# Two-layer trunk of delta rule, attention and convolution: convolution in pieces, a second home for the masked coupling, memory values with tokens stationary

## The reference, cut to what matters

```python
h = rms_norm(x, norm_pre[layer])
qkv_a, z_a, b_a, g_a, q_b, k_b, v_b, z_b = split_sizes(h @ w_in, AB_SIZES)
qkv_a = silu(causal_depthwise_conv(qkv_a, conv_w))          # 4 taps
# delta rule, chunks of 64 tokens:
n_mat = where(strict, (k_beta @ k.T) * gamma, 0)             # the coupling within a chunk
sol = triangular_solve(eye + n_mat, rhs)                     # u and w
# over the 8 chunks, one after the other:
v_new = u_i - w_i @ state
o = qd_i @ state + qk_i @ v_new
state = state * cd_i + kd_i.T @ v_new
# memory: m = rms_norm(mem, mem_norm[layer]); k, v = split(m @ w_kv, 2)
```

## Time and profile before

| what | value |
|---|---|
| median of 3 runs | 2610.19 us |
| lowest and highest run | 2605.46 and 2610.9 us |
| the profiled execution | 2604.95 us |
| its span, first to last instruction | 2603.2 us |
| mean granted TensorE clock | 0.984 |
| busy share of PE, DVE, ACT, POOL | 95%, 51%, 31%, 12% |

### The profile page before, as it was taken

The page is one execution under the profiler, slowest core; times in us unless marked ns, Lnnn a source line. Parts: engine busy times, 40 slices in busy tenths (PEclk is TensorE's granted clock), DMA queues, the critical chain, the costliest instruction groups (busy, mean ns, idle before and its releaser), DMA issues.

```text
span 2603.2 us, 30751 instructions
## 1 busy us (share of the span) xinstructions
PE 2475.8 (95%) x12244; PEld 2055.0 (79%) x12244; DVE 1315.7 (51%) x1689; ACT 808.6 (31%) x1348; POOL 299.5 (12%) x198
## 2 busy tenths in 40 slices
PE   7999998999999999989989989999999999999986
PEld 6788787878887777978877778888888888887765
DVE  5555545554355656763355575333433343433746
ACT  4232322223244345542233441122212222322442
POOL 3010110202011011001121140000000000010304
PEclk9999999999999999999999989999999999999997
DMA  9522322156355332443321222323232322332212
GB/s 173 88 57 49 66 50 68 45 56 65 51 129 90 65 89 65 154 161 130 96 84 63 76 81 92 101 75 116 91 100 78 114 92 92 98 98 96 73 50 80
DMA packets 222976, 227.76 MB, mean 87 GB/s; under 512 B 9360, under 2 KB 216464, under 8 KB 222864
## 3 DMA queue, kind: packets, MB, share of 16 engines
q1 hardware_dynamic: 222720, 225.64, 34.5%
q10 hardware_dynamic: 144, 0.52, 0.1%
HBM read 221.94 MB, written 4.19 MB: 87 GB/s over the span
## 4 chain that ended last, share of the span: by engine, by line
PE 64%; issue 24%; DVE 5%; POOL 3%; ACT 1%; DMA 1%; SPq 1%; POOLq 0%; ACTq 0%; DVEq 0%
PE acc L797 20%; PE acc L799 19%; PE acc L798 19%; POOL work L1782 2%; DVE weights_lo L1145 1%; DMA weights_raw<-in_ab_w_in 1%; DVE work L1548 1%; PE m L941 1%; PE m L1086 1%; PE m L1098 1%; POOL small L1759 0%; ACT work L719 0%; PE m L1021 0%; DVE input_lo L1561 0%; PE m L776 0%
## 5 line engine op out<-in xcount | busy, mean ns | idle before, releaser
L797 PE MATMUL acc<-input_hi,weights_hi 128*128 128x512 f32 (+1 forms) x3168 | 1242.6, 392 | 53.0 <-DVE weights_lo L1145 22.4
L799 PE MATMUL acc<-input_hi,weights_lo 128*128 128x512 f32 (+1 forms) x3168 | 1214.8, 383 | 1.8 <-issue 1.8
L798 PE MATMUL acc<-input_lo,weights_hi 128*128 128x512 f32 (+1 forms) x3168 | 1213.1, 383 | 0.0
L797 PEld LDWEIGHTS acc<-input_hi,weights_hi 128*128 128x128 f32 x3168 | 601.3, 190 | 188.8 <-issue 35.7
L1145 DVE TENSOR_TENSOR weights_lo<-weights_raw,weights_hi 128x1024 fp32r<-128x1024 f32 x400 | 534.8, 1351 | 374.2 <-ACT weights_hi L409 373.0
L799 PEld LDWEIGHTS acc<-input_hi,weights_lo 128*128 128x128 f32 x3168 | 600.4, 190 | 117.2
L798 PEld LDWEIGHTS acc<-input_lo,weights_hi 128*128 128x128 f32 x3168 | 601.9, 190 | 109.5 <-issue 1.9
L409 ACT ACTIVATE weights_hi<-weights_raw 128x1024 fp32r<-128x1024 f32 x400 | 418.5, 1057 | 617.9 <-PE acc L799 576.9
L1821 POOL TENSOR_TENSOR work<-work 128x512 f32<-128x512 f32 x56 | 72.6, 1296 | 429.0 <-ACT work L671 425.0
L1759 POOL TENSOR_TENSOR small<-small 128x4 f32<-128x4 f32 (+1 forms) x20 | 25.5, 1275 | 741.7 <-DVE small L1329 382.8
L1527 DVE COPY work<-acc 128x512 f32<-128x512 f32 x64 | 41.6, 686 | 134.8 <-PE acc L799 121.6
(11 more groups left out here) (240 smaller groups left out, 1864.9 us busy)
## 6 DMA issues: line engine op xcount, KB each, us to landing
weights_raw<-in_ab_w_in SPq DMA_DIRECT2D x128, 512.0 KB, 5.3
weights_raw<-in_c_w_in SPq DMA_DIRECT2D x128, 512.0 KB, 3.7
weights_raw<-in_m_w_kv SPq DMA_DIRECT2D x32, 512.0 KB, 3.4
weights_raw<-in_ab_w_out SPq DMA_DIRECT2D x32, 512.0 KB, 4.5
weights_raw<-in_m_w_q SPq DMA_DIRECT2D x32, 512.0 KB, 3.3
weights_raw<-in_c_w_out SPq DMA_DIRECT2D x32, 512.0 KB, 3.9
residual<-in_x SPq DMA_DIRECT2D x32, 256.0 KB, 5.2
weights_raw<-in_m_w_o SPq DMA_DIRECT2D x16, 512.0 KB, 3.3
```

What stands on the lines that cost most here:

```text
L797: pe.matmul(out, w_hi[:, o:o + P], hi(kt), start=kt == 0, stop=False)
L798: pe.matmul(out, w_hi[:, o:o + P], lo(kt), start=False, stop=False)
L799: last = pe.matmul(out, w_lo[:, o:o + P], hi(kt), start=False, stop=kt == last_kt)
```

## The change: what it does, and the diff

Six edits go together.
- `convolve` takes its k step: scale and first tap behind step 0, one shifted tap behind each of the steps 1, 2 and 3, always after the replies of that step; the gate of the tile before comes behind step 3. ScalarE's tanh moves one chunk later and to step 1.
- The hops of the delta rule are spread over slots 12 to 60 in place of 12 to 63. `tr`, `dk`, `qb` and `p0` keep their slots (12, 16, 21, 23), `p1` and `y1` go from 26 and 27 to 25 and 26, `y4` and `p5` from 36 and 38 to 35 and 36, `r4` and `s4`, which shared 52, to 49 and 50, `s7` from 59 to 56 and `ft` from 63 to 60.
- The masked coupling is written in turn to `c_t` and to `gam`, which is free once `qb`'s reply has used it. Level 1 now waits for that reply (`qk`), level 2 for `y0`, a later level s for the matmuls of `p` two levels back.
- `value_chunk` projects the values with the memory's tokens as the stationary operand and 256 weight columns moving, so that they come out with tokens on partitions; the transposes and both VectorE copies go.
- ScalarE's `take_values` copies the values to `mv`, scaled by each token's factor: 8 activations in all, ahead of the rest of chunks 12, 16 and 28 and after the last one.
- VectorE's `take_keys` keeps the keys' part.

```diff
@@ -124,3 +124,3 @@
 B_REPLY = {"vt": 1.2, "a": 0.8, "a00": 2.0, "a10": 2.0, "b": 1.2, "b03": 1.8, "b13": 1.8, "f": 0.6}
-D_SLOTS, B_SLOTS = weighted(D_HOPS, 12, 63, D_REPLY), weighted(B_HOPS, 18, 63, B_REPLY)
+D_SLOTS, B_SLOTS = weighted(D_HOPS, 12, 60, D_REPLY), weighted(B_HOPS, 18, 63, B_REPLY)
 C_REPLY = {"s": 5.0, "t": 1.8, "o": 1.5}
@@ -264,2 +264,3 @@
         halves = lambda t: t.rearrange("p (t a n) -> p t a n", a=2, n=CH)
+        level = lambda s: (c_t, gam)[s % 2]
         wq_q = wq.rearrange("p (t n) -> p t n", n=4 * CH)[:, :, CH:3 * CH]
@@ -583,3 +584,3 @@
 
-                    if c == 2:
+                    if c == 3:
                         EA.round(it)
@@ -594,8 +595,8 @@
 
-                    if 1 <= like <= 4 and c < 2:
-                        tanh_conv(it - 1, 2, c)
-                    if like < 4 and c in (8, 9):
-                        tanh_conv(it, 0, c - 8)
-                    if like < 4 and c in (12, 13):
-                        tanh_conv(it, 1, c - 12)
+                    if 1 <= like <= 4 and c in (1, 2):
+                        tanh_conv(it - 1, 2, c - 1)
+                    if like < 4 and c in (9, 10):
+                        tanh_conv(it, 0, c - 9)
+                    if like < 4 and c in (13, 14):
+                        tanh_conv(it, 1, c - 13)
 
@@ -620,3 +621,3 @@
                             projected(c)
-                        if k == 3:
+                        if k == 1:
                             convolved(c)
@@ -652,4 +653,17 @@
 
+            def take_values(q):
+
+                l, j, pair = q // 4, q % 4, P_KV + q
+                act.wait_ge(chunk_used, done_at(pair))
+                act.wait_ge(acc_free, 2 * pair)
+                act.wait_ge(*MG("pow"))
+                for m in range(2):
+                    v0 = (l * 2 + m) * MH * HD + 256 * (j - 2)
+                    act.activation(mv[:, v0:v0 + 256], bank(pair, m, 256), ACT.Copy, scale=t2[:, m:m + 1])\
+                        .then_inc(acc_free, 1)
+
             for c in range(32):
                 split(C_KV + c + 1)
+                if c in (12, 16, 28):
+                    take_values(c // 4 - 1)
                 if 1 <= c <= 8:
@@ -662,2 +676,3 @@
                     split_input(0, xt, C_OUT0, c - 24, c - 23)
+            take_values(7)
 
@@ -871,4 +886,5 @@
                     pe.wait_ge(*GV("y" + str(int(name[1]) - 1), i))
+                    c_s = level(int(name[1]))
                     for h, t in ht:
-                        last = pe.matmul(m(m01, h, t), c_t[:, o(h, t)], inv[:, o(h, t)], start=True, stop=True)
+                        last = pe.matmul(m(m01, h, t), c_s[:, o(h, t)], inv[:, o(h, t)], start=True, stop=True)
                 elif name[0] == "y":
@@ -981,8 +997,20 @@
 
-            def value_transposes(l, j, pair):
+            def value_chunk(g, pair, kt0, l, between):
 
-                pe.wait_ge(*MV(f"vf{l}{j}"))
-                for n in range(4):
-                    last = pe.transpose(acc[2 * (pair % 2)][:, n * P:(n + 1) * P], v_feat[:, n * P:(n + 1) * P], ident)
-                last.then_inc(*MM.did(f"v{l}{j}"))
+                s = g % SPLIT_SLOTS
+                pe.wait_ge(lo_ready, g + 1)
+                if kt0 == 0:
+                    pe.wait_ge(acc_free, 2 * (pair - 1))
+                for k in range(4):
+                    kt = kt0 + k
+                    w = slice(s * CW + k * 256, s * CW + (k + 1) * 256)
+                    for m in range(2):
+                        out = bank(pair, m, 256)
+                        tok = slice(m * P, (m + 1) * P)
+                        pe.matmul(out, mem_h(H_hi, l, kt)[:, tok], w_hi[:, w], start=kt == 0, stop=False)
+                        pe.matmul(out, mem_h(H_hi, l, kt)[:, tok], w_lo[:, w], start=False, stop=False)
+                        last = pe.matmul(out, mem_h(H_lo, l, kt)[:, tok], w_hi[:, w], start=False, stop=kt == KT - 1)
+                    if k == 3:
+                        last.then_inc(chunk_used, 1)
+                    between(k)
 
@@ -1003,3 +1031,3 @@
             for c in range(32):
-                l, q = c // 16, c // 4 - 1
+                l = c // 16
 
@@ -1009,5 +1037,6 @@
                             attn(name, 3)
-                if q >= 0 and c % 4 == 1 and q % 4 >= 2:
-                    value_transposes(q // 4, q % 4, P_KV + q)
                 mem_rms(c)
+                if c % 16 >= 8:
+                    value_chunk(C_KV + c, P_KV + c // 4, 4 * (c % 4), l, between)
+                    continue
                 chunk(C_KV + c, P_KV + c // 4, 4 * (c % 4), KT - 1, width=MEM, between=between,
@@ -1015,3 +1044,2 @@
                       hi=lambda k: mem_h(H_hi, l, k), lo=lambda k: mem_h(H_lo, l, k))
-            value_transposes(1, 3, P_KV + 7)
 
@@ -1337,3 +1365,3 @@
 
-            def convolve(it, sec, n):
+            def convolve(it, sec, n, k):
 
@@ -1342,10 +1370,13 @@
                 tap = lambda k: pcol("a_conv", (8 * sec + 2 * it + n) * 4 + k)
-                dve.wait_ge(chunk_used, ab_done(pair))
-                TTO(conv_in, bank(1 + sec, n), rs[:, :], ALU.mult).then_inc(acc_free, 1)
-                dve.wait_ge(acc_free, 2 * pair + n + 1)
-                TS(dst, conv_in, tap(3), None, ALU.mult).then_inc(*EV.did())
-                for d in (1, 2, 3):
+                if k == 0:
+                    dve.wait_ge(chunk_used, ab_done(pair))
+                    if n:
+                        dve.wait_ge(*EV.last())
+                    TTO(conv_in, bank(1 + sec, n), rs[:, :], ALU.mult).then_inc(acc_free, 1)
+                    dve.wait_ge(acc_free, 2 * pair + n + 1)
+                    TS(dst, conv_in, tap(3), None, ALU.mult).then_inc(*EV.did())
+                else:
                     dve.wait_ge(*EV.last())
-                    STT(out=dst[:, d:T], in0=conv_in[:, 0:T - d], scalar=tap(3 - d), in1=dst[:, d:T],
-                        op0=ALU.mult, op1=ALU.add).then_inc(*EV.did(f"c{sec}{n}" if d == 3 else None))
+                    STT(out=dst[:, k:T], in0=conv_in[:, 0:T - k], scalar=tap(3 - k), in1=dst[:, k:T],
+                        op0=ALU.mult, op1=ALU.add).then_inc(*EV.did(f"c{sec}{n}" if k == 3 else None))
 
@@ -1381,10 +1412,10 @@
 
-            def evacuate(it, like, sec, c):
+            def evacuate(it, like, sec, c, k):
 
                 if like < 4:
-                    if c:
-                        gate(it, sec, c - 1)
                     if c < 2:
-                        convolve(it, sec, c)
-                elif c < 2:
+                        convolve(it, sec, c, k)
+                    if c and k == 3:
+                        gate(it, sec, c - 1)
+                elif c < 2 and k == 0:
                     keep(it, sec, c)
@@ -1426,5 +1457,3 @@
 
-                    if like and c < 3:
-                        evacuate(it - 1, like - 1, 2, c)
-                    if c == 2:
+                    if c == 3:
                         EV.round(it)
@@ -1441,5 +1470,2 @@
                         decays()
-                    for sec, at_ in ((0, 8), (1, 12)):
-                        if at_ <= c < at_ + 3:
-                            evacuate(it, like, sec, c - at_)
                     if like == 0 and c == 8:
@@ -1447,2 +1473,10 @@
 
+                def evacuated(c, k):
+
+                    if like and c < 3:
+                        evacuate(it - 1, like - 1, 2, c, k)
+                    for sec, at_ in ((0, 8), (1, 12)):
+                        if at_ <= c < at_ + 3:
+                            evacuate(it, like, sec, c - at_, k)
+
                 for c in range(16):
@@ -1453,2 +1487,4 @@
                         projected(c)
+                        for k in range(4):
+                            evacuated(c, k)
                         continue
@@ -1471,20 +1508,10 @@
 
-            def take_kv(q, c):
+            def take_keys(q):
 
                 l, j, pair = q // 4, q % 4, P_KV + q
-                if c == 0:
-                    dve.wait_ge(chunk_used, done_at(pair))
-                    for n in range(2):
-                        if j < 2:
-                            TTO(mkt(l, 2 * j + n), bank(pair, n, MEM), rs[:, 0:MEM], ALU.mult).then_inc(acc_free, 1)
-                        else:
-                            TTO(v_feat[:, n * MEM:(n + 1) * MEM], bank(pair, n, MEM), rs[:, 0:MEM], ALU.mult)\
-                                .then_inc(*MV.did(f"vf{l}{j}"))
-                elif c == 2 and j >= 2:
-                    dve.wait_ge(*MM(f"v{l}{j}"))
-                    for n in range(2):
-                        h = 2 * (j - 2) + n
-                        dst = mv[:, l * 2 * MH * HD:(l + 1) * 2 * MH * HD].rearrange("p (m h n) -> p m h n", m=2, h=MH)
-                        dve.tensor_copy(dst[:, :, h, :], bank(pair, 0)[:, n * MEM:(n + 1) * MEM].rearrange(
-                            "p (m n) -> p m n", m=2)).then_inc(acc_free, 1)
+                dve.wait_ge(chunk_used, done_at(pair))
```

(14 more changed lines are left out.)

6 lines of the change are left out of this document (3 added, 3 removed).

## The result

| | before | after |
|---|---|---|
| median of 4 runs, us | 2609.07 (2605.46 to 2610.9) | 2578.02 (2575.1 to 2580.61) |
| profiled execution, its span | 2604.95, 2603.2 | 2578.57, 2576.8 |
| rounds 1 to 4 (chunks 16 to 79) | 592.98 | 566.19 |
| memory phase (chunks 128 to 159) | 126.02 | 122.98 |

After over before is 0.9882 [0.9865, 0.9899]. The change is faster, as forecast: the profiled execution came down by 26.4 us where the sum said 25.7.

The account below looks back on a forecast made before the run. TensorE, busy for 95% of the span, was taken as the bound: its instruction stream plus idle time. Terms -14.4 - 7.0 + 5.2 - 4.0 - 1.1 - 4.4 = -25.7 gave 2584.5 us against the median of 2610.19; range 2574 to 2598.

Parts of the forecast that it names:

- rival B: `p5` costs nothing and both stalls at the turn of the rounds' loop go; 2577.5 us, chance 0.10.
- The signs that were named: Waits before `s` and `p1` gone, new `p5` wait, no 2 us turn stall; rounds about 21 less, memory phase 3 to 5.
- `s`, -14.4: Convolution in pieces and hops spread anew remove all 14 waits before `s`: -14.4 us, at worst -7 if half comes back.
- `p1`, -7.0: Second home for the masked coupling removes the 1.76 us wait before `p1` in all four rounds: -7.0 us.
- `p5`, +5.2: With one k step less after `y4`, `p5` waits 1.3 us for VectorE in four rounds: +5.2 us, between 0 and +6.
- The turn, -4.0: 18 matmuls, 4.3 us, behind `ft` cover the rounds' loop turn's first stall; second stall left: -4.0 us, between 0 and -5.8.
- Tanh, -1.1: ScalarE's split goes ahead of its tanh in chunk 1 of round 4, ending TensorE's wait: -1.1 us.
- The memory phase, -4.4: Values projected with tokens stationary: sixteen transposes and their waits go, ScalarE's copies are covered; -4.4 us, between -2 and -5.
- C: Rival: convolution pieces delay every hop of the recurrence, 0.85 us at 48 hops; slower, 2625.3 us, chance 0.04.
- D: Rival: waits before `s` and `p1` are replaced by equal ones, `p5`'s above all; 2608 us, chance 0.06.
- A: Rival: the recurrence keeps half its waits before `s` and the loop's turn its stall; 2595.5 us, chance 0.18.
- E: Rival: POOL's mask and VectorE's `y0` hold each other, `p1` 1.22 us later per round; 2589.4 us, chance 0.05.

Follow-up runs that it names:

- run 1: Kernel before with only the convolution in pieces and ScalarE's tanh moved, hops still over slots 12 to 63; 2595.93 us, rounds 580.79.
- run 5: Changed kernel with the hops spread over slots 12 to 63 again; 2584.18 us, rounds 572.7.
- run 6: Changed kernel with the convolution in one place again and the tanh move undone, hops still over 12 to 60; 2594.58 us, rounds 583.4.
- run 2: Kernel before with only the second home for the masked coupling; 2603.02 us, rounds 585.17.
- run 7: Changed kernel with `p5` in slot 37 in place of 36 and `y5` in 38 in place of 37; median 2570.86 us, rounds 562.01.
- run 9: Kernel before, unchanged, profiled once more; 2609.99 us, memory phase 128.71.
- run 3: Kernel before with only the memory's values projected with tokens stationary; 2605.04 us, memory phase 122.83.
- run 8: Changed kernel with `ft` in slot 62 in place of 60; 2585.17 us, rounds 572.17.
- run 12: Kernel of run 7 with every hop from `qb` to `s7` one slot later, `ft` still in 60; median 2580.58 us, rounds 573.5.

## Why the prediction was right, point by point

- **The number.** The median, 2578.02, is 6.5 below the forecast of 2584.5 and almost on rival B's 2577.5. The number alone would speak for B; the waits speak for the forecast, since `p5` does wait, and B had it for nothing. The signs that were named came true except one: the rounds shrank by 26.8, not by about 21.
- **`s`, -14.4: right.** All 14 waits went. Runs 1 and 5 show which part does it: the pieces take 10.1, the slots to 60 the 4.3 of `s4` and `s6`. For `s4` the prediction said so; that `s6` needed the new slots too, since a split stands ahead of its reply, it didn't see. The lower end, half coming back, didn't happen; run 6 shows that 13.6 would have come back, had the slots been narrowed without the pieces.
- **`p1`, -7.0: right** (7.0 of idle time in run 2; its rounds shrank by 7.8, but its turns were 1.1 shorter too). The room at the new slot was seen right as well: 0.20 in the prediction, 0.17 in after.
- **`p5`, +5.2: right, measured 4.5.** The wait stands where it was put, four times 1.13 to 1.15, not 1.3. It was needless: run 7 moves two slots and has it back, 4.2 us of the rounds.
- **The turn, -4.0: too small.** Both stalls went, 2.10 + 1.90 and twice 0.9, but for 0.24, so 5.6. The step that failed is "the second I leave, since it comes from instructions that arrive late after the branch": the second stall went with 6 matmuls behind `ft` already, and no run shows where it comes from. Half of rival B's case was true; its other half (`p5` for nothing) wasn't. The argument for the 4.0, that 18 matmuls cover 2 us by their length of 4.3, came out right by luck: 12 matmuls, 2.8 us, are longer than the stall too and cover nothing.
- **Tanh, -1.1: right**; that wait of the earlier trace rows is gone.
- **What the sum lacked: about 3 us in the rounds.** By idle time the terms come to -14.4 - 7.0 - 5.6 - 1.1 + 4.5 = -23.6; the rounds shrank by 26.8. In the rows a wait costs more than its idle time. In the earlier trace rows `p1` starts 1.76 after the modelled end of the matmul before it, which is 0.39 long; but matmuls that don't wait start 0.23 apart (313.99 and 314.22 in after), so 0.16 is lost beside the idle time. After a wait the four matmuls of `s` take 0.55 to the next group (243.43 to 243.98 in the trace of before) and 0.44 without (243.56 to 244.00). That makes 0.16 to 0.27 for each wait; with 23 gone and 4 new, 3.0 to 5.1. The 3.2 found is at the lower end. This is worked out, not shown: run 1, with 7 waits fewer, gains 2.0 beyond its idle time, but run 7, with the four of `p5` gone, gains its 4.2 of idle time and nothing beyond.
- **The memory phase, -4.4: measured -3.0 in the two profiled executions, 5.6 to 5.9 where the clock falls alike.** Chunk by chunk: -1.1 at chunk 156; -4.3 at the last chunk, of which about 1.5 is clock (before has a half-clock stretch at 1153.4 that after hasn't; a last value chunk of the new form takes 4.8 with one, 3.3 without); -0.4 twice for the transposes without a wait; +0.4 for a new wait for a low part before chunk 146. Without the clock that is -4.3, what was said. The +2.7 in chunks 128 and 129 is clock (run 9), and not the change. Where the clock falls alike in chunks 128 and 129, the phase shrinks by 5.6 (before to run 6), 5.9 (run 1 to run 6) and 5.7 (run 9 to after). The 1.5 may belong to the change after all: all five executions with the transposes have a half-clock stretch over the last value chunk, and three of the nine without them. Then the term was too small by 1.2 to 1.5. One reading in it is wrong beside this: of the copies that VectorE loses it says that no one waited for them, but the last two groups of transposes waited for them.
- **The total: close by luck.** The sum and the measurement differ by only 0.7 in the profiled execution because the rounds gave 5.5 more than forecast (26.8 against 21.3), the memory phase 1.4 less, and the rest of the program grew by 3.4, where nothing was forecast: +1.0 in chunks 0 to 7, +1.6 in chunks 216 to 231. The change edits nothing there. The 1.6 goes with the clock, as at chunk 129: the five executions in which chunks 216 to 231 take 96.7 us (after, runs 3, 5, 6 and 8) have a separate half-clock stretch of 3.4 us that begins behind the wait for the input's low part 10 us into them, and after's wait there is 3.08. In the nine with 95.1 to 95.2 us there is no such stretch, and before's wait is 1.21. For the other 1.8 no run shows the cause. The medians differ by 31.05, since the profiled execution of before lay 4.1 below its median and after's 0.6 above.
- **The bounds.** The prediction has its own case span 2577 to 2594. By the bounds of its terms the upper end is 2610.2 - 7 - 7.0 + 6 - 0 - 1.1 - 2 = 2599.1, just outside the range; the measurement doesn't test it.
- **C and D** find nothing for them: at `r` and `s` VectorE waits for TensorE, not the other way. **A** would have left 7 in `s`. **E** is refuted where it was put, but only since the mask (to 312.96) is all but done when L1285 starts (312.82, for 1.23); run 12 shows its price where two such instructions do meet, 2.05 a time.
